# Hybrid HGRN2/attention/pooling layer on one core: gates by tanh, and the branch inputs split on two other engines

## What is computed

```python
def _head_rms_norm(o, g):
    o = o * lax.rsqrt(jnp.mean(jnp.square(o), -1, keepdims=True) + RMS_EPS)
    return o.reshape(B, T, -1).astype(g.dtype) * g
...
    y_l = _head_rms_norm(ol_f + flip(ol_b), norm_g) * jax.nn.silu(gl)      # branch A (HGRN2)
...
def _merge_branches(u, ys, w_branch, w_out):
    z = jnp.einsum('btjc,jcd->btjd', jnp.stack(ys, axis=2), w_branch)
    gates = jax.nn.sigmoid(u[..., COL_GATE:].reshape(B, T, N_BRANCH, D_MODEL))
    return jnp.sum(gates * z, axis=2) @ w_out
...
    ul = (xl * (1 + sc1_l) + sh1_l) @ w_in
    ya_l = _hgrn_mixer(...); yc_l = _attention_mixer(...); yb_l = _pool_mixer(...)
    xl = _layer_norm(ALPHA * xl + g1_l * _merge_branches(ul, (ya_l, yb_l, yc_l), w_branch, w_out), ln1_g, ln1_b)
    xl = _layer_norm(ALPHA * xl + g2_l * _sq_relu_mlp(xl * (1 + sc2_l) + sh2_l, w_ff1, w_ff2), ln2_g, ln2_b)
```

## Time and profile before

| | us |
|---|---|
| median of 3 runs | 2015.3 (2012.96 to 2015.35) |
| the profiled execution | 2018.67, of which the span from first to last instruction is 2016.9 |
| TensorE busy (matmuls) | 1905.7, mean granted clock 0.976 of full speed |
| VectorE busy | 1267.5 |
| ScalarE busy | 784.7 |
| GpSimd busy | 439.9 |

### The profile page before, as it was taken

The page is one execution under the profiler, slowest core; times in us unless marked ns, Lnnn a source line. Parts: engine busy times, 40 slices in busy tenths (PEclk is TensorE's granted clock), DMA queues, the critical chain, the costliest instruction groups (busy, mean ns, idle before and its releaser), DMA issues.

```text
span 2016.9 us, 26285 instructions
## 1 busy us (share of the span) xinstructions
PE 1905.7 (94%) x10808; PEld 1634.5 (81%) x10808; DVE 1267.5 (63%) x1419; ACT 784.7 (39%) x898; POOL 439.9 (22%) x335
## 2 busy tenths in 40 slices
PE   6899899999898989999999999999999999999996
PEld 1478787889888867777778887997899899889975
DVE  1345656785666575667867666767566556556686
ACT  1221224454544545544344444533333333333332
POOL 0000000003727322023421000246045005302510
PEclk8999999999999999999999999899999999999998
DMA  9956554454333244456666674465665556656552
GB/s 401 421 199 225 215 197 175 169 188 168 105 126 111 98 159 144 147 173 265 229 234 248 263 257 167 185 242 179 229 230 218 200 209 223 212 192 225 217 180 89
DMA packets 59320, 409.05 MB, mean 203 GB/s; under 512 B 6336, under 2 KB 9024, under 8 KB 10304
## 3 DMA queue, kind: packets, MB, share of 16 engines
q1 hardware_dynamic: 54720, 395.34, 53.4%
q10 hardware_dynamic: 4480, 12.02, 1.6%
HBM read 405.24 MB, written 2.10 MB: 202 GB/s over the span
## 4 chain that ended last, share of the span: by engine, by line
PE 71%; DVE 13%; DMA 4%; DVEq 3%; issue 3%; POOL 3%; ACT 2%; POOLq 0%; SPq 0%; ACTq 0%
PE main L1292 12%; PE main L1294 12%; PE main L1293 12%; PE main L1253 9%; PE main L1254 9%; PE main L1255 9%; DVE asum L863 5%; DVE wlo L842 4%; DMA raw<-in_w_in 2%; DVEq L862 2%; DMA raw<-in_w_ada 2%; PE side L1324 1%; ACT whi L399 1%; PE side L1483 1%; PE main L1343 1%
## 5 line engine op out<-in xcount | busy, mean ns | idle before, releaser
L842 DVE TENSOR_TENSOR wlo<-raw,whi 128x1024 fp32r<-128x1024 f32 x552 | 742.4, 1372 | 414.3 <-ACT whi L399 413.8
L399 ACT CAST whi<-raw 128x1024 fp32r<-128x1024 f32 x552 | 571.8, 1050 | 854.6 <-PE main L1294 349.1
L1253 PE MATMUL main<-h,whi 128*128 128x256 f32 x1024 | 291.4, 285 | 4.1 <-DVE h L1160 2.1
L1254 PE MATMUL main<-h,whi 128*128 128x256 f32 x1024 | 291.0, 284 | 0.0
L1255 PE MATMUL main<-h,wlo 128*128 128x256 f32 x1024 | 290.9, 284 | 0.0
L1253 PE MATMUL main<-hCL,whi 128*128 128x256 f32 (+1 forms) x800 | 264.6, 331 | 14.0 <-DVE wlo L842 3.8
L1254 PE MATMUL main<-hCL,whi 128*128 128x256 f32 (+1 forms) x800 | 260.5, 326 | 0.0
L1255 PE MATMUL main<-hCL,wlo 128*128 128x256 f32 (+1 forms) x800 | 260.2, 325 | 0.0
L863 DVE SCALAR_TENSOR_TENSOR asum<-raw,sm,asum 128x512 f32<-128x512 f32 x240 | 200.9, 837 | 19.7 <-issue 0.9
L1292 PE MATMUL main<-whi,hid 128*128 128x512 f32 x512 | 201.9, 394 | 5.1 <-DVE wlo L842 4.4
L1253 PEld LDWEIGHTS main<-h,whi 128*128 128x128 f32 x1024 | 197.9, 193 | 4.8 <-DVE h L1160 2.5
(11 more groups left out here) (229 smaller groups left out, 2674.3 us busy)
## 6 DMA issues: line engine op xcount, KB each, us to landing
raw<-in_w_f SPq DMA_DIRECT2D x128, 1024.0 KB, 5.0
raw<-in_w_in SPq DMA_DIRECT2D x108, 1024.0 KB, 5.0
raw<-in_w_ada SPq DMA_DIRECT2D x96, 1024.0 KB, 7.0
raw<-in_w_br SPq DMA_DIRECT2D x24, 1024.0 KB, 6.9
raw<-in_w_out SPq DMA_DIRECT2D x16, 1024.0 KB, 5.0
xin<-in_xT SPq DMA_DIRECT2D x4, 1024.0 KB, 19.9
ax<-in_xtok ACTq DMA_DIRECT2D x1, 2048.0 KB, 8.0
lng<-in_rows ACTq DMA_DIRECT2D x2, 1024.0 KB, 5.8
```

Source lines behind the costliest of these rows:

```text
L399: nc.scalar.copy(whi[:, q % 4], slots[slot][:, 2 * h:2 * h + 2]).then_inc(hi_made, 1)
L842: TT(wlo[:, q % 4], slots[slot][:, 2 * h:2 * h + 2], whi[:, q % 4].bitcast(F32), ALU.subtract).then_inc(lo_made, 1)
L1253: mm(out, w_hi, x_hi, start=start, stop=False)
L1254: mm(out, w_hi, x_lo, start=False, stop=False)
```

## The change

1. Sigmoid is replaced by `tanh` of half the argument: sigmoid(x) = (1 + tanh(x/2)) / 2. ScalarE takes tanh with scale 0.5, VectorE computes (tanh + 1) times the other factor in one `scalar_tensor_tensor`, and the factor 1/2 goes into `inverse_rms` (the mean square is scaled by 4) for branch A, and into `merged_hi` and `merged_lo` for the merged sum.
2. Tables are asked for: `exp_and_others` at the start of mix and behind each `inverse_rms`, and `natural_log_exp_and_others` ahead of each. Tanh and the exponential share a table, and so do the logarithm and exponential of `inverse_rms`.
3. `two_parts` for the branches is gone from GpSimd. ScalarE makes the high part (`branch_high`), VectorE the low one (`branch_low`), with a new count `y_hi`. GpSimd's pooling work waits for `at_o` 8 in place of `at_y` 8.

```diff
             def inverse_rms(i):
+                nc.scalar.preload_act_table_set("natural_log_exp_and_others")
                 act.wait_ge(o_ms, i + 1)
-                A(o_r[i], side[:, 0:2].rearrange("p a (c b) -> p (a c) b", b=T), ACT.Ln, scale=1.0 / HD, bias=RMS_EPS)
+                A(o_r[i], side[:, 0:2].rearrange("p a (c b) -> p (a c) b", b=T), ACT.Ln, scale=4.0 / HD,
+                  bias=4.0 * RMS_EPS)
                 drain()
                 A(o_r[i], o_r[i], ACT.Exp, scale=-0.5).then_inc(o_rs, 1)
+                nc.scalar.preload_act_table_set("exp_and_others")
...
+            nc.scalar.preload_act_table_set("exp_and_others")
             for i in range(2):
...
-                            A(ya[:, i * 4 + b], main[:, b, 0:T], ACT.Sigmoid).then_inc(gs_sig, 1)
+                            A(ya[:, i * 4 + b], main[:, b, 0:T], ACT.Tanh, scale=0.5).then_inc(gs_sig, 1)
...
+            def branch_high(j):
+                act.wait_ge(*((y_done, 2), (at_y, 8), (pool_y, 8))[j])
+                nc.scalar.copy(yR[j % 2][:, :, 0], (ya, cq, xb)[j]).then_inc(y_hi, 1)
...
-                    A(sg[:, t], main[:, t], ACT.Sigmoid).then_inc(freed["A"], 1)
+                    A(sg[:, t], main[:, t], ACT.Tanh, scale=0.5).then_inc(freed["A"], 1)
...
+                    if h == 0 and k == 1:
+                        branch_high(0)
...
+                    if pp == 0 and k == 0:
+                        branch_high(1)
-                    if pp == 0 and k == 1:
+                    if pp == 0 and k == 2:
                         act.wait_ge(y_lo, 2)
                         act.dma_start(g1b, spread(R_BG1).rearrange("p (a b) -> p a b", b=C)).then_inc(g1_ld, 16)
...
+            branch_high(2)
             act.dma_start(ax[:], xtok).then_inc(ax_ld, 16)
...
-                nc.scalar.copy(mR[:, 4 * pp:4 * pp + 4, 0], src).then_inc(m_hi, 1)
+                nc.scalar.mul(mR[:, 4 * pp:4 * pp + 4, 0], src, 0.5).then_inc(m_hi, 1)
...
-            pool.wait_ge(y_done, 2)
-            two_parts([yR[0][:, :, n] for n in range(2)], ya, y_lo)
             rotate(1)
             pool.wait_ge(at_o, 4)
             group_values(1)
-            pool.wait_ge(at_y, 8)
+            pool.wait_ge(at_o, 8)
             drain()
-            two_parts([yR[1][:, :, n] for n in range(2)], cq, y_lo)
...
-            pool.wait_ge(pool_y, 8)
-            two_parts([yR[0][:, :, n] for n in range(2)], xb, y_lo)
...
-                            TT(ya[:, i * 4 + b], ya[:, i * 4 + b], main[:, b, 0:T],
-                               ALU.mult).then_inc(freed["V"], 1)
+                            STT(ya[:, i * 4 + b], ya[:, i * 4 + b], 1.0, main[:, b, 0:T], ALU.add,
+                                ALU.mult).then_inc(freed["V"], 1)
...
+            def branch_low(j):
+                dve.wait_ge(y_hi, j + 1)
+                TT(yR[j % 2][:, :, 1], (ya, cq, xb)[j], yR[j % 2][:, :, 0].bitcast(F32),
+                   ALU.subtract).then_inc(y_lo, 1)
...
+                    if h == 0 and k == 1:
+                        branch_low(0)
...
+                    if pp == 0 and k == 1:
+                        branch_low(1)
...
+                    if pp == 0 and k == 1:
+                        branch_low(2)
```

More of the change, by code:

```diff
@@ L323, in build @@
          lv_exp, lv_op, lv_sc, lv_cp, vg_in, o_exp, o_op, o_ps, o_sq, o_ms, o_rs, y_done, gs_sig, at_sw, at_rot,
-         at_v, at_sc, at_max, at_exp, at_norm, at_tr, at_cp, at_o, at_y, y_lo, pool_diff, pool_ps, pool_y, m_done,
+         at_v, at_sc, at_max, at_exp, at_norm, at_tr, at_cp, at_o, at_y, y_hi, y_lo, pool_diff, pool_ps, pool_y, m_done,
          m_tr, m_hi, m_lo, ax_in, var_in, rs_out, nm_out, h2_tr, h2_hi, h2_lo, x1_done, hid_lo, y_out, cleared) = (
@@ L329, in build @@
             "lv_exp lv_op lv_sc lv_cp vg_in o_exp o_op o_ps o_sq o_ms o_rs y_done gs_sig at_sw at_rot "
-            "at_v at_sc at_max at_exp at_norm at_tr at_cp at_o at_y y_lo pool_diff pool_ps pool_y m_done "
+            "at_v at_sc at_max at_exp at_norm at_tr at_cp at_o at_y y_hi y_lo pool_diff pool_ps pool_y m_done "
             "m_tr m_hi m_lo ax_in var_in rs_out nm_out h2_tr h2_hi h2_lo x1_done hid_lo y_out cleared").split())
@@ L1045, in branch_out @@
                     if j == 0:
-                        TT(m_t[:, t, cols(pp)], sg[:, t], main[:, 2 + t], ALU.mult).then_inc(freed["V"], 1)
+                        STT(m_t[:, t, cols(pp)], sg[:, t], 1.0, main[:, 2 + t], ALU.add,
+                            ALU.mult).then_inc(freed["V"], 1)
                     else:
@@ L1050, in branch_out @@
                             dve.wait_ge(m_done, n - 1)
-                        TT(gz[:, 2 * t:2 * t + 2], as_rows(sg[:, t]), as_rows(main[:, 2 + t]),
-                           ALU.mult).then_inc(freed["V"], 1)
+                        STT(gz[:, 2 * t:2 * t + 2], as_rows(sg[:, t]), 1.0, as_rows(main[:, 2 + t]),
+                            ALU.add, ALU.mult).then_inc(freed["V"], 1)
             for h in range(2):
@@ L1094, in merged_lo @@
                 src = side[:, 2 * (pp % 2):2 * (pp % 2) + 2].rearrange("p a (c b) -> p (a c) b", b=T)
-                TT(mR[:, 4 * pp:4 * pp + 4, 1], src, mR[:, 4 * pp:4 * pp + 4, 0].bitcast(F32),
-                   ALU.subtract).then_inc(m_lo, 1)
+                STT(mR[:, 4 * pp:4 * pp + 4, 1], src, 0.5, mR[:, 4 * pp:4 * pp + 4, 0].bitcast(F32),
+                    ALU.mult, ALU.subtract).then_inc(m_lo, 1)
             for pp in range(4):
```

## The result

The changed kernel takes 2008.96 us in the median of 13 runs (2000.71 to 2013.93), beside 2021.02 for the kernel before in 13 runs (2012.96 to 2029.79). The ratio is 0.9931, 95% interval 0.9908 to 0.9954: faster by 0.69%, or 13.9 us of 2021.02 (the two medians themselves are 12.1 us apart). The forecast was 1998.9 us, 16.4 us less than 2015.3, with a range of 1992 to 2007; the time lies 2 us above the range. One run of dead_reads, a kernel further down, took 6613.95 us; that kernel's median and ratio here are those of its other eleven runs.

The account below looks back on a forecast made before the run. The prediction took TensorE's work plus its holes to bound the kernel. Gains of 2.6 + 7.1 + 3.3 + 3.4 = 16.4 us from a median of 2015.3 gave 1998.9 us, with an 8-in-10 range of 1992 to 2007.

Parts of the forecast that it names:

- its lower bound: Mix's removed sigmoid table load gains nothing if another chain, such as levels starting from GpSimd's arguments, is as late.
- part 3: Branch inputs leave GpSimd, so VectorE's pairs shorten and TensorE's holes close: 7.1, 3.3 and 3.4 us at branches 0, 1, 2.
- The edits touch nothing that decides: Rival, chance 0.04: weight loads made VectorE late at the three branch entries; only mix's 2.6 us is gained, 2012.7 us.
- the added work lands in the holes: Rival, chance 0.04: pairs at branch entries stay at 5 to 9 us, holes grow by the new subtraction; slower, 2022.6 us.
- Part 1: Tanh for sigmoid in mix removes a 1.28 us table load from the last chain in both rounds: 2.6 us.
- a sign of being wrong: In mix, the level loop's waits on TensorE grow by what the removed table load gave.
- Part 2: The other table loads, at the gates and inverse_rms, are hidden behind ScalarE's waits; removing them gains 0 us.
- The constant inside the VectorE instruction: Adding 1 within scalar_tensor_tensor is free, 0 us; a rival, chance 0.02, had it taking twice as long, 2008.5 us.
- Branches 0 and 1, 7.1 + 3.3: Closed holes of 4.4 and 1.88 us at the two entries, plus low clock behind them of 2.8 and 1.4 us.
- Branch 2, 3.4 us: At its entry VectorE's pair ends sooner, closing TensorE's holes of 2.50 and 0.95 us.
- The sum: Whole kernel: 2.6 + 7.1 + 3.3 + 3.4 = 16.4 us gained.
- The base: Whole kernel: 2015.3 us, the median of the runs shown, from which the 16.4 us gain was taken to reach 1998.9.

Follow-up runs that it names:

- before_again: The kernel before, run again without an edit for a second trace; 2018.75 us (profiled).
- split_only: The kernel after with sigmoids, tables and factors as before, so only the branch inputs move to ScalarE and VectorE; 2006.93 us, ratio to before 0.994.
- tanh_only: The kernel after with GpSimd still making the branch inputs, so only tanh, the factor and the tables change; 2020.62 us, ratio to before 1.0012.
- after_again: The kernel after, run again without an edit; 2006.55 us, ratio to before 0.9944.
- after_3: The kernel after, run once more without an edit, on the same chip as the combined rotations; 2004.59 us, ratio to before 0.9935.

## Why the load in mix was worth nothing

Read the chain that ended last around the second round's gate, before and then after (start, us, what). The kernel after is later by the start; TensorE's scores of the level ahead of this place begin at 619.37 and at 628.11, so the shift between the traces is 8.7 us.

```profile
620.20 1.28 ACT L547
...
628.44 1.10 DVE lv L975
...
629.59 2.07 PE side L1483 x16
...
631.73 1.54 POOL lv L720
...
638.97 0.02 ACT lv L536
```

```profile
628.82 1.19 ACT ya L552 x4
...
636.02 1.77 DVE lv L984
...
637.83 2.07 PE side L1505 x16
...
639.97 2.00 POOL lv L734
...
647.68 0.02 ACT lv L541
```

With the shift off, the gate starts at 620.1, where the load stood. VectorE's level step starts at 627.3, 1.1 us sooner than before, but takes 1.77 us, not 1.10; the scores start at 629.1, only 0.5 us sooner. GpSimd's first argument then takes 2.00 in place of 1.54 us, and the next exponential starts where it did (638.97 and 647.68, again 8.7 us apart). The timeline of GpSimd gives the reason, before and then after:

```profile
621.50 1.15 POOL L720 TENSOR_TENSOR lv<-lf 128x512 f32<-128x512 f32 x1 [3.27 <-PE side L1483]
...
625.86 2.13 POOL L723 TENSOR_TENSOR lv<-lf,lfk 128x512 f32<-128x512 f32 x1
```

```profile
630.24 1.16 POOL L734 TENSOR_TENSOR lv<-lf 128x512 f32<-128x512 f32 x1 [3.27 <-PE side L1505]
...
635.55 1.14 POOL L737 TENSOR_TENSOR lv<-lf,lfk 128x512 f32<-128x512 f32 x1
```

GpSimd's four arguments start at 621.50 in both, the shift off: they hang on the scores of another level, which the load does not touch. Before, they ended at 628.0, just ahead of VectorE's step at 628.44. Now VectorE's step starts at 636.02 inside GpSimd's last (to 636.7) and waits for it. That the levels started from GpSimd's arguments may be as late stood in the prediction as its lower bound. The waits of TensorE say the same in sum: for the gate and the levels 2.2 + 18.8 = 21.0 us in before, before_again and split_only, and 20.4 to 21.4, all of it for the levels, in the nine kernels and repeats with tanh that leave mix's level loop as it is (tanh_only, after, after_again, after_3, dead_reads, dead_writes, rot_early, rot_both, rot_both_2). The wait was handed on.

What is left of a difference in mix goes with the clock. From level 2's scores to attention's first ones TensorE's granted clock was at the 1.2 GHz level for 10.2 us in before_again, and the stretch takes 199.0 us. With 17.1 to 17.7 us at that level it takes 200.9 in before, 200.9 in split_only, 200.8 in tanh_only and 200.7 in after_3. With 20.5 to 21.0 it takes 201.3 to 201.5 in after, after_again, dead_reads and dead_writes. At like clock the kernels with and without the loads are within 0.3 us, and the time at the low clock doesn't go by the loads: the two executions of before have 17.1 and 10.2 us of it. Two experiments test the two strands further.

**extra_loads** puts two loads ahead of each of mix's tanh groups, 2.56 us per round. **half_args** lets GpSimd write zeros for two of the four arguments of a level.

```diff
 extra_loads
                     if k == 3:
+                        nc.scalar.preload_act_table_set("natural_log_exp_and_others")
+                        nc.scalar.preload_act_table_set("exp_and_others")
 half_args
-                TT(q[:, :, 0], w[:, :, 0], w_mid, ALU.subtract)
-                TT(key[:, :, 0], f_mid, fk[:, :, 0], ALU.subtract)
+                nc.gpsimd.memset(q[:, :, 0], 0.0)
+                nc.gpsimd.memset(key[:, :, 0], 0.0)
```

> The changed kernel with two table loads (2.57 us) back ahead of the tanh of branch A's gate, in each round, where the kernel before had one ahead and one behind the weight chunk. Theory E (a delay here is taken up within two levels, because every second level waits for GpSimd's arguments of the other parity): the first load is taken up as before, and of the second at most 1.28 us is left per round; mix's part of the trace from level 2's scores to the last scores of the second round grows by 0 to 2.6 us from 161.0. Rival (each load is worth its length): it grows by 5.1 us.

> The changed kernel, with two of GpSimd's four instructions per level replaced by memsets of the same halves (these arguments are left out: the levels get zeros there). It measures what GpSimd's arguments cost the level loop. Theory F (the loop is bound by GpSimd's arguments, 6 to 7.7 us a level with what VectorE holds them up): TensorE's waits for the level operands, 20.5 us in nine, fall under 5 us, and mix's stretch of 161.0 us shrinks by 15 us or more with the low clocks behind the waits. Rival (the loop is bound by VectorE's and ScalarE's order of steps, splits ahead of operands): waits stay above 10 us.

Measured, one execution each: extra_loads 1999.72 us (its start was an early one, 505.0), with mix at 162.7 us where the kernel after has 160.4 to 161.1. Four loads of 1.28 us, 5.1 in all, cost 1.6 to 2.3 at the very place where I had valued two at their full length, within theory E's 0 to 2.6 (its 161.0 us, too, ends at level 7's scores). Mix is no finer test than that: with no load there dead_reads and dead_writes (below) have 162.1 us. Up to attention's first scores extra_loads takes 201.8 us with 20.5 us at the low clock, 0.2 to 0.5 more than the four kernels with as much of it. The waits show it too:

```profile
PE side L1507 <- DVE lv L986: 16.5, 7, 3.5
...
PE main L1277 <- DVE ya L1035: 4.8, 2, 2.4
```

(TensorE's waits in extra_loads.) The gate's wait grows to 4.8 us, the levels' shrinks to 16.5, and the sum is 21.3 us again.

half_args is the opposite case. It takes 1984.8 us, with mix at 145.2 us: 15.9 less than the kernel after, with the same instructions on ScalarE and VectorE. The waits of TensorE for the levels in half_args:

```profile
PE side L1505 <- DVE lv L984: 10.1, 4, 3.8
```

They halve, from 20.5 us, and don't vanish: in four of the levels TensorE still waits up to 3.8 us for VectorE. Of theory F the 15 us came and the waits under 5 us did not; at 10.1 us they are just over the rival's 10. So GpSimd's arguments carry much of the pace of mix and not all of it. How they do it stays open: a fill reads nothing, and so VectorE's products of the levels, too, got faster (21.9 us in eighteen, 28.6 in the kernel after), while GpSimd's steps went from 99.6 to 64.2 us. The experiment doesn't part the two.

## Is it the port that GpSimd and VectorE share?

The gain of the split says that VectorE is slow beside GpSimd's two steps. It doesn't say through what: the two also read and write SBUF side by side, and GpSimd's steps delayed the second rotation. Both kernels here are the kernel after with dead work put on GpSimd where `two_parts` for `ya` had stood, into a buffer that isn't yet in use. dead_reads does the same two steps as before (two reads and a write), dead_writes three fills (writes only).

```diff
 dead_reads
+            pool.wait_ge(y_done, 2)
...
+            TT(yR[1][:, :, 0], xb, one, ALU.mult)
+            drain()
+            TT(yR[1][:, :, 1], xb, yR[1][:, :, 0].bitcast(F32), ALU.subtract)
...
             rotate(1)
 dead_writes
+            pool.wait_ge(y_done, 2)
+            for n in range(3):
+                nc.gpsimd.memset(yR[1]..., 0.0)
...
             rotate(1)
```

> The changed kernel with two dead GpSimd instructions back in their old place at branch 0's entry: a product and a difference on 128x2048 elements, read from xb and ones and written where nothing reads them before it is overwritten. Nothing waits for them but the second rotation, 50 us later. Theory A (a GpSimd instruction that reads two SBUF operands holds up VectorE's two-operand instructions until it ends): VectorE's pair behind the subtraction takes 7 to 10 us again, TensorE's wait of 4 to 5 us for attention's exponential is back, ratio to the changed kernel 1.002 to 1.004. Rival C (the hole was there because of what GpSimd's steps made, or because TensorE waited for their result): nothing changes.

> The changed kernel with three dead GpSimd memsets of 128x4096 elements in the same place, about as long together as the two removed steps. They read nothing. Theory A: VectorE's pairs take 2.4 us, no wait for attention's exponential, time as the changed kernel. Rival D (any GpSimd instruction that uses SBUF slows VectorE): the pair is long and the hole is back, as with the dead products.

Measured: dead_reads 2010.66 us, ratio to before 0.9961 (0.9942 to 0.998), 1498.7 us from level 2's scores to the end, some 5 us more than the kernel after. dead_writes 2002.46 us, ratio 0.9926 (0.99 to 0.9952), 1492.5 us, no more than it. The timelines of GpSimd and then VectorE in dead_writes:

```profile
707.70 10.82 POOL L780 MEMSET yR<- 128x4096 f32 x3 [0.73 <-DVE ya L1012]
```

```profile
707.57 2.34 DVE L856 TENSOR_TENSOR wlo<-raw,whi 128x1024 fp32r<-128x1024 f32 x2
```

And in dead_reads, GpSimd and then VectorE:

```profile
717.83 10.12 POOL L780 TENSOR_TENSOR yR<-xb,ones 128x2048 fp32r<-128x2048 f32 x1 [1.83 <-DVE ya L1013]
728.09 4.51 POOL L782 TENSOR_TENSOR yR<-xb,yR 128x2048 fp32r<-128x2048 f32 x1
```

```profile
717.66 2.35 DVE L857 TENSOR_TENSOR wlo<-raw,whi 128x1024 fp32r<-128x1024 f32 x2
719.93 2.28 DVE L1057 TENSOR_TENSOR yR<-ya,yR 128x2048 fp32r<-128x2048 f32 x1
722.14 2.35 DVE L857 TENSOR_TENSOR wlo<-raw,whi 128x1024 fp32r<-128x1024 f32 x2
...
728.28 4.60 DVE L1102 TENSOR_SCALAR pr<-pr,col 128x512 f32<-128x512 f32 x1
...
738.33 0.49 DVE L1102 TENSOR_SCALAR pr<-pr,col 128x512 f32<-128x512 f32 x1
```

Fills on GpSimd for 10.8 us leave VectorE's subtractions at 2.34 us. Reads hold one of the two engines, and which one depends on who is first. In dead_reads VectorE began 0.17 us ahead, and did its three steps (five instructions) at full speed, until 724.49: it is GpSimd's product that took 10.12 us, where it had taken 5.65 and takes 3.60 undisturbed (before, branches 1 and 2). So it did not get in between VectorE's instructions either, but lost the whole 6.5 us. The pairs that I had expected to grow did not, and the wait for attention's exponential did not come back. Then GpSimd's second step held VectorE's scaling of `pr`, 0.49 us by itself, for 4.60 us; TensorE waited 3.63 us for it, on its timeline in dead_reads:

```profile
732.94 0.66 PE L1565 MATMUL side<-cs,pr 128*128 128x128 f32 x4 [3.63 <-DVE pr L1102]
```

So the mechanism stands, though theory A named the wrong engine as the one that waits at the first step. The 5 us that the two dead steps cost are within its ratio of 1.002 to 1.004. No data are shared. A shared bandwidth doesn't fit: fills of as long a time cost nothing, and of two engines that read, one keeps its full speed. One engine stands still while the other's instruction with reads runs. The Trainium skill (SBUF — State Buffer, "SBUF: two separate sides") has it so: the pair of ports is an exclusive lock, taken for a whole instruction by whoever comes first, and a VectorE instruction with two SBUF inputs meets it only against a GpSimd instruction that reads SBUF. The trace agrees on both points, 2.35 beside 10.12 us and 2.34 beside fills. The held scaling has only one array as its input, besides a column of factors. The same sentence names a second sort of VectorE instruction that takes the pair, one in a 2-port perf mode. That the scaling is of this sort no run here shows by itself; it fits that alone it takes 0.49 us, where a two-operand step on as many elements takes 0.69.

## What was left: the rotations

TensorE waits 2.38 us for GpSimd's first rotation and 2.45 us behind the second. **rot_early** does the products of the first rotation in place during the last chunks of mix, with ScalarE's swap of halves moved there; only its last sum waits for its buffer. **rot_both** also moves the second swap behind a chunk's exponential.

```diff
 rot_early
+                    if i and k == 9:
+                        act.wait_ge(vg_in, 2)
+                        swap(0)
...
-            act.wait_ge(vg_in, 2)
-            swap(0)
...
+                TT(g4, g4, cos4, ALU.mult)
+                TT(qs[:], qs[:], sin4, ALU.mult)
+                drain()
+                TT(ak[:, h, C:], ks[:, 0], ks[:, 1], ALU.add)
+                pool.wait_ge(o_ps, 2)
+                TT(qr[:], g4, qs[:], ALU.add).then_inc(at_rot, 1)
 rot_both, besides
-                    if h == 0 and k == 8:
-                        act.wait_ge(at_rot, 1)
-                        swap(1)
...
+                    if h == 0 and k == 9:
+                        act.wait_ge(at_rot, 1)
+                        swap(1)
```

> The changed kernel with the first rotation earlier: ScalarE's swap stands at chunk 9 of mix's second round, GpSimd multiplies cq in place and adds into qr once the outputs are made. Theory A says that the wait of 2.4 us for POOL ak at branch 0's entry goes, with the low clock behind it where there is one: 2.4 to 4 us less, ratio to before 0.9925. Rival: GpSimd's products now hold up VectorE in mix's last chunks, and a wait of like size appears there: no gain.

> As rot_early, and the second swap stands behind chunk 9's work and not in chunk 8, so that the second rotation lies beside VectorE's idle time between the two halves of attention. Theory A: the hole of 2.45 us for DVE pr (780.33 in the changed kernel) goes too, with the low clock behind it: 2.5 to 4 us less than rot_early. Rival: the rotation ends too late for the first scores of the second half, and TensorE waits there instead.

> Both rotations moved, again, beside the changed kernel. Theory A: from the scores of level 2 to the end 1486 us within 2 (1486.1 in the first trace), 0.4% under the changed kernel, ratio to before 0.990. Rival: the first result was a chip in a good hour, and it lies with the changed kernel at 0.994.

| | time, us | ratio to before, 95% | level 2's scores to end |
|---|---|---|---|
| rot_early | 2002.24 | 0.9923, 0.9895 to 0.9951 | 1489.5 |
| rot_both | 1996.33 | 0.9905, 0.9875 to 0.9934 | 1486.1 |
| rot_both_2 (the same kernel) | 1997.01 | 0.9897, 0.9877 to 0.9916 | 1486.2 |

Against the 1493.6 us that the kernel after takes in the mean of three, the first rotation gives 4.1 us and the second another 3.4. The two gaps were 4.8 us. The other 2.7 fit the clock: behind them the kernel after has 0.50 from 719 to 722 us and 0.57 from 780 to 784, and rot_both has 1.00 from 675 to 1230. Beside after_3, whose 2004.59 us were taken on the same chip as rot_both_2, the version is 7.6 us faster, and it beats both kernels of this study. Of the waits in branch 0 only one is left on TensorE's timeline in rot_both, up to branch 1's 1.28 us:

```profile
776.55 1.99 PE L1587 MATMUL side<-prT,avg 128*128 128x256 f32 x8 [0.30 <-ACT prT L589]
...
912.12 0.50 PE L1330 MATMUL main<-whi,hCL 128*128 128x512 f32 x1 [1.28 <-DVE wlo L867]
```

## Why the prediction was right and wrong

- **The mechanism and the sign: right.** GpSimd's two steps held VectorE, and the gain is that of part 3. The pairs fell to 2.35 and 2.36 us, the gaps of 4.38, 1.88, 2.50 and 0.95 us are gone. The rival "The edits touch nothing that decides" would have left the split without a gain; split_only gives it all. The rival "the added work lands in the holes" needed pairs over 5 us with GpSimd idle.
- **Part 1, 2.6 us: the step that failed.** "TensorE was already waiting for the gate ... and stays in wait behind it ..., so there is room for the whole of it", and so the load was taken at its full 1.28 us in each round. It was worth nothing: tanh_only is no faster than before. The chain had the load in it, but the level loop has two strands that take turns, and the other is as late: what was won moved VectorE's step into GpSimd's, and within one level it was gone. The gate's wait of 2.2 us did vanish, and the levels' rose by 1.7 (by 1.6 to 2.6 in the other runs); the prediction had named that as a sign of being wrong. A piece of the chain that ended last is worth what the next chain leaves of it.
- **Part 2: right.** Ten table loads fewer, the two of part 1 among them, bring no time: tanh_only is at 1.0012 (0.9993 to 1.003). The constant inside the VectorE instruction has no price that could be seen either.
- **Branches 0 and 1, 7.1 + 3.3 = 10.4 us:** split_only gains 10.9 us there, the kernel after 9.4 to 9.6. The difference is clock: the kernel after has one more low stretch, told below. Set instruction against instruction, TensorE in the first trace of the kernel after makes up 7.1 us on before over branch 0's gap and the low clock behind it, and 3.8 over branch 1's, and loses 1.6 at attention's first scores. The first is the 7.1 of the forecast, the second 0.5 more than its 3.3, and the loss was not in it.
- **Branch 2, 3.4 us:** 5.0. A third gap of 0.34 us closed with the two, and TensorE's idle time from 1036 to 1060 us went from 3.8 us to none. A gap also costs more than its idle time: the matmuls on either side of the three start 2.89, 1.34 and 0.73 us apart, where 0.23 is the step without a gap, and the step behind the first matmul is 0.34 in place of 0.23. That makes 4.6 us for the three, and the forecast had counted idle time alone. The 0.9 us in the rest were not in the sum either, and the change has no part in them that shows: split_only has them, tanh_only and dead_reads don't. They fit the clock around the layer norm's gap, 0.53 over 10 us before, 0.91 and 0.75 over two such stretches after (rows below).
- **The return of 1.2 us ahead of attention** was not in it either. It isn't the tanh's: dead_reads and dead_writes have 39.2 and 39.4 us there (and 162.1 in mix). Around level 7's scores the granted clock is 0.83 in before and 0.67 in the kernel after (ten us each; TensorE alone: width, busy, granted clock, DMA share, GB/s).

```profile
669.00:679.00 10.00, 9.21 (x64) 0.83 0.53 195
```

```profile
678.00:688.00 10.00, 9.44 (x56) 0.67 0.52 191
```

- **The sum** from level 2's scores on: forecast 16.4, measured 13.9. Part 1 took 2.6 from it, mix 0.3 more and the return ahead of attention 1.2, both with the clock, branches 0 and 1 0.9; branch 2 and the rest gave 1.6 and 0.9 more. That it lies only 2.5 us off is partly luck, since the misses have both signs.
- **The base: the other step that failed.** Because "the holes should be the same in both", the forecast took 2015.3, a median of three, for its base, and so came to 1998.9 us. The kernel before has 2021.02 in 13 runs, 5.7 us more: the larger part of the miss of 10.1 us. From 2021.0, the same sum gives 2004.6, and a range as wide would have held the 2008.96: it was the base, more than the sum, that put the time 2 us outside. The three runs shown spread by 2.4 us and hid a start that moves by more. The profiled execution beside them, 2018.67, was a hint, and I took its distance for chance.

```profile
1260.00:1270.00 10.00, 6.99 (x31) 0.53 0.56 210
```

```profile
1250.00:1260.00 10.00, 4.74 (x28) 0.91 0.34 121
1260.00:1270.00 10.00, 9.90 (x65) 0.75 0.48 171
```

(TensorE alone, of before and then of after: width, busy, granted clock, DMA share, GB/s.)

## What to carry to other kernels

Where an elementwise instruction of VectorE with two operands in SBUF takes several times its own length, look what GpSimd runs at that moment; giving GpSimd's large two-operand steps to ScalarE and VectorE can pay even though the busier engines get more work. An item in the chain that ended last can be worth anything from nothing to its length: before it is counted in full, follow the strand that runs in turns with it, and see whether the work that moves up lands beside the other engine's instructions. Base a forecast of less than 1% on a stretch that repeats, or on more than three runs.

## What the runs showed of the hardware

**The start's clock varies from execution to execution.** In thirteen profiled executions (half_args has other work in the first levels) level 2's scores come between 504.7 and 517.5 us, though the programs are alike up to there but for one table load. The three earliest, up to 505.1, have a granted clock of 0.94 or 0.95 over the first 250 us, the latest 0.88. Single executions of the kernel after go from 2000.71 to 2013.93 us, as far apart as the change is worth, and starts differ by as much. What sets the clock I have not found out.

**A gap of 2.4 us sometimes costs a low clock and sometimes not.** At attention's first scores TensorE waits 2.38 to 2.57 us in all of these kernels but those with the rotations moved. Timelines of TensorE, tanh_only and then split_only:

```profile
711.11 2.07 PE L1545 MATMUL side<-ak,qr 128*128 128x512 f32 x2 [2.38 <-POOL ak L765]
```

```profile
711.93 1.13 PE L1545 MATMUL side<-ak,qr 128*128 128x512 f32 x2 [2.39 <-POOL ak L765]
```

The same two instructions take 2.07 or 1.13 us. The kernel after is of the first sort, and its stretches behind 720.0 (width; busy PE, granted clock, DMA share, GB/s) show 1.2 GHz for the first 2 us:

```profile
720.00:722.00 2.00, 2.00 (x5) 0.50 0.88 360
722.00:724.00 2.00, 2.00 (x9) 0.94 0.21 86
```

Before, before_again, split_only, dead_reads, dead_writes and extra_loads are of the sort without, tanh_only, after, after_again and after_3 of the sort with it; in half_args the clock falls 1.3 us behind the start of these scores. As dead_reads, dead_writes and extra_loads have the tanh, tanh alone is not the cause, and what is stays open.
